# A two-block transformer kernel: raw rows for three units behind each norm of the second block, bias products, another order of PSUM banks

## The chip, the cores and the metric

One Trainium2 chip, one of its cores. The metric is the device time of one launch in microseconds (us), lower is better. All arithmetic is float32; large matrix products are made of float32r products.

## The reference, cut to what matters

A first block (sparse attention, convolution branch, feed-forward network) is followed by a second block of two layers, over 512 tokens of width 1024. The change concerns the norm at the head of each layer of the second block:

```python
for layer in range(2):
    mod = silu(c) @ ada_w[layer] + ada_b[layer]
    shift, scale, gate = split(mod, 3)
    h = rms_norm_2(x, norm_w[layer]) * (1 + scale) + shift
    proj = h @ w_in          # even layer: q, k, v, gates, latents; odd layer: q, k, v, gates
    y = mixer(proj)          # even: two attentions; odd: windowed attention with sinks
    x = x + gate * y
```

For layer 0, `x` is itself the final rms_norm of the first block. Since the inverse root is one number per token, `h @ W` is also `r * ((x * g) @ W) + shift @ W`, with `g` the product of norm weight and `1 + scale` and `r` the inverse root of the token.

## The kernel before, in words

Activations lie transposed: 128 channels on the partitions, 512 tokens along the free axis, eight chunks for the width of 1024 (`xT`). A weight matrix is cut into units of 128 output columns. The list `UNITS` (171 of them) is the order in which SyncE loads them (512 KB each) into five slots of `raw`; the load of a unit waits until the unit five places ahead is done. GpSimd splits each one into `whi` (rounded to float32r) and `wlo` (the rest). TensorE works out a unit in `unit` (L427): for each of eight chunks k a piece of three products of 128x128 by 128x512 (whi by hi, whi by lo, wlo by hi), all into one PSUM bank, 24 products a unit. So the moving side has to be there as a pair hi, lo as well: for the norms `hhi` and `hlo`.

A norm runs over four engines. ScalarE squares each chunk (`square`, L1015, two buffers), VectorE adds the squares up (`add_square`, L1467), TensorE sums them over partitions with `ones` (`sums_of`, L475, one-column products), VectorE and ScalarE make the inverse root (`inverse_root`, L1446; `root`, L1034), TensorE spreads it over the partitions (`spread`, L492), and then VectorE and ScalarE make the rows: `h_split` (L1477) multiplies chunk and gain by the spread root into a PSUM bank (L1485), ScalarE adds the shift and rounds it to `hhi` (`h_high`, L1040), VectorE writes the remainder to `hlo` (L1496). The first unit behind the norm asks for row k before piece k.

Norm "e" of layer 0 stands behind the last "down" products (L687) of the feed-forward network: `double_sums` (L704) sums two vectors, "f" and "e", because the final norm of the first block and the norm of layer 0 are worked out together (VectorE L1915 to L1918 joins them). Four units with their norms on latents follow: ("ecq", 0), ("ecq", 1), ("eckv", 0), ("ekr", 0); then ("eq", 0..3), ("ek", 0), ("ev", 0), ("ega", 0..2), and a loop of 32 attention steps with units as filling (the first is ("ega", 3)). The loop's scores are L773. Tables for the rotary embedding and the latents' matrices (L1265, L1266) are loaded by ScalarE's queue when the last "down" unit is done, and the first rope waits for all of them.

Norm "o" of layer 1 stands behind the eight units "eout". VectorE adds each of them to `xT` (`residual`, L2055) and the squares are added up at once. Then come ("oq", 0..7), ("ok", 0..1), ("ov", 0..1), ("og", 0), and a loop of windowed attention (scores L889) with ("og", 1..7) as filling.

A PSUM bank is taken on TensorE by `Banks.take`: each pool (a tuple of banks) has its own counter, and the next taking of a pool gets the next bank of the tuple; it waits until the last user of that bank, of whatever pool, has freed it. Units use the pool `WIDE` = (0, 1, 2, 3) where nothing else is said: 34 of them before norm "e", 13 between it and the attention loop, then ("eout", 3..7), the "o" units and ("og", 0). ("eout", 0..2) use the pool (0, 1, 2); the scores of both loops (1, 2); the filling units (0,) in the first loop and (0, 3) in the second; sums and spreads `TR` = (4, 5); the rows of h 6 and 7.

The core lines of such a piece, with their order:

```python
for part, (w, x) in enumerate(((whi, hi), (whi, lo), (wlo, hi))):
    m = mm(b[:, :], w[:, s, k * P:(k + 1) * P], x, start=..., stop=...)
```

Of the kernel before, what the change touches and what calls it, by code (L numbers as in the profile page):

```python
# [21 lines left out]
P = 128  # L22
# [89 lines left out]

ROOTS = ("n1", "fe", "o", "z")
# [67 lines left out]
def program(nc, d, out, known):  # L181
    found = {}
    ctx = ExitStack()
    with ctx:  # L184
# [44 lines left out]
        sb("arena_rest", [AB - NR])  # L229
# [82 lines left out]
        sinT = area(T)  # L312
        esg = chunks(area(8 * T), 8)
# [16 lines left out]
        sgr, ropet = hs[:, 0, :], hs[:, 1, :]  # L330

# [86 lines left out]
        def _(pe):  # L418
# [8 lines left out]
            def unit(name, i, src=h_parts, first=None, inline=True, pool=WIDE):  # L427
# [5 lines left out]
                def piece(k):  # L433
# [15 lines left out]
                return piece  # L449

# [24 lines left out]
            def sums_of(name, b, at=0):  # L475

                last = sqt[:, known.get(("sqslot", (name, DC - 1)), 0), :]
                pe.wait_ge(*dve_did.at((name, "acc", DC - 2)))
                for src in (sq_sum[name], last):
                    if src is last:  # L480
                        pe.wait_ge(*sq_ready.at((name, DC - 1)))
                    for tt in range(TT):
                        m = mm(b[:, at + tt:at + tt + 1], src[:, tt * P:(tt + 1) * P], ones[:, 0:1],  # L483
                               start=(src is not last and at + tt == 0), stop=(src is last), skip_group_check=True)
                return m

            def sums_once(name, pool=TR):

                b = bank.take(pe, pool, (name, "sum"))
                sums_of(name, b).then_inc(*pe_did.up((name, "sum")))  # L490
# [213 lines left out]
            def double_sums():  # L704

                b = bank.take(pe, (0,), ("fe", "sum"))
                for half, name in enumerate(("f", "e")):
                    m = sums_of(name, b, half * TT)
                m.then_inc(*pe_did.up(("fe", "sum")))
# [8 lines left out]
            double_sums()  # L718


            spread("e", 0, at=TT)
            spread("f", 0)
# [1566 lines left out]
```

## Time and profile before

| | us |
|---|---|
| median of 3 runs (lowest, highest) | 1392.66 (1387.76, 1399.45) |
| the profiled execution | 1388.33 |
| its span, first to last instruction | 1386.5 |
| mean granted clock of TensorE | 0.98 of 2.4 GHz |

PE is TensorE's products, PEld its weight loads, DVE VectorE, ACT ScalarE, POOL GpSimd, SP SyncE. A row of a timeline gives start, duration, engine, line, operation, output and inputs, shapes and count; in brackets stands the idle time of the engine before it and what ended that. A matmul's duration contains its latency; products follow each other more closely than their durations say. A one-pass product has one record; a float32 product by `ones` or `ident` has two.

### The profile page before, as it was taken

To read this page: it belongs to the slowest core of one execution; us is meant where nothing else is said; L and a number is where in the kernel's file an instruction comes from. 1 tells how busy PE (TensorE), PEld (TensorE's weight loads), DVE (VectorE), ACT (ScalarE), POOL (GpSimd) and SP (SyncE) were. 2 spreads that over 40 slices of the span, in tenths; PEclk is the share of its full clock that TensorE was granted. 3 is DMA by queue.
4 is the path that set the end of the run, shared out by engine and by line. 5 is a ranking of instruction groups with operands and counts; after the bars stand their busy time and mean duration, and the time that the engine had idled before them with its cause. 6 is when DMAs were issued, how large, how long until landed. Compare 5 with 4: busy or idle time off the path is not lost. (4 is left out here: it accounts for less than half of the span.)

```text
span 1386.5 us, 19493 instructions
## 1 busy us (share of the span) xinstructions
PE 1327.6 (96%) x7206; PEld 1040.8 (75%) x7206; DVE 792.5 (57%) x1534; ACT 415.6 (30%) x907; POOL 640.0 (46%) x523
## 2 busy tenths in 40 slices
PE   7999999999999999999999989999999979999996
PEld 6888776688888888888788768776556858766675
DVE  3996778924554777777562354536654251155643
ACT  3011355523121211221110231246665121244521
POOL 5774422236675666666576355632000446622230
PEclk9999999999999999999999989999999989999998
DMA  6431111122353455555543142210000212211111
GB/s 232 149 95 49 59 31 32 31 62 84 99 167 122 159 205 183 198 197 184 180 152 102 46 148 92 76 47 31 1 1 1 82 60 92 91 31 47 32 46 61
DMA packets 37377, 130.23 MB, mean 94 GB/s; under 512 B 4400, under 2 KB 4656, under 8 KB 37040
## 3 DMA queue, kind: packets, MB, share of 16 engines
q1 hardware_dynamic: 27072, 94.16, 21.6%
q10 hardware_dynamic: 10224, 34.94, 6.8%
q8 instruction: 58, 0.95, 0.3%
q14 instruction: 23, 0.19, 0.1%
HBM read 126.98 MB, written 2.10 MB: 93 GB/s over the span
## 5 line engine op out<-in xcount | busy, mean ns | idle before, releaser
L974 POOL TENSOR_TENSOR wlo<-raw,whi 128x1024 fp32r<-128x1024 f32 x171 | 417.6, 2442 | 14.3
L970 POOL TENSOR_TENSOR whi<-raw,ones 128x2 fp32r<-128x2 f32 x171 | 43.1, 252 | 696.1 <-DMA raw<-in_w 696.0
L442 PE MATMUL bank<-hhi,whi 128*128 128x512 f32 x648 | 267.4, 413 | 11.1 <-DVE hlo L1496 4.8
L442 PE MATMUL bank<-ysplit,whi 128*128 128x512 f32 x896 | 277.4, 391 | 0.0
L442 PE MATMUL bank<-hhi,wlo 128*128 128x512 f32 x648 | 255.7, 395 | 0.0
L442 PE MATMUL bank<-hlo,whi 128*128 128x512 f32 x648 | 255.5, 394 | 0.0
L442 PEld LDWEIGHTS bank<-ysplit,whi 128*128 128x128 f32 x896 | 168.2, 188 | 35.8 <-issue 0.8
L971 POOL TENSOR_SCALAR whi<-raw 128x1022 fp32r<-128x1022 f32 x171 | 185.2, 1083 | 0.0
L442 PE MATMUL bank<-ysplit,wlo 128*128 128x512 f32 x448 | 174.7, 390 | 0.0
L442 PEld LDWEIGHTS bank<-hhi,whi 128*128 128x128 f32 x648 | 123.3, 190 | 49.7 <-issue 13.6
L442 PEld LDWEIGHTS bank<-hhi,wlo 128*128 128x128 f32 x648 | 123.5, 191 | 27.2
L442 PEld LDWEIGHTS bank<-hlo,whi 128*128 128x128 f32 x648 | 124.1, 192 | 21.7
L1529 DVE SCALAR_TENSOR_TENSOR arena<-first,arena 128x512 f32<-128x512 f32 x120 | 119.3, 1032 | 0.9
L442 PEld LDWEIGHTS bank<-ysplit,wlo 128*128 128x128 f32 x448 | 84.2, 188 | 17.6
L1220 ACT ACTIVATE arena<-bank,cols 128x512 f32<-128x512 f32 x44 | 34.3, 779 | 177.7 <-DVE bank L1834 177.7
L687 PE MATMUL bank<-hhi,whi 128*128 128x512 f32 x176 | 69.9, 397 | 5.5 <-DVE modp L1818 3.3
L1992 DVE CUSTOM_DVE_ANT_0 arena<-bank,arena 128x512 f32<-128x512 f32 x64 | 44.2, 690 | 48.4 <-PE bank L778 28.9
L1030 ACT ACTIVATE sqt<-xbuf 128x512 f32<-128x512 f32 x40 | 25.3, 632 | 152.0 <-DVE xbuf L2058 72.5
L1329 ACT ACTIVATE arena<-arena,nmax,stat 128x512 f32<-128x512 f32 x64 | 51.6, 807 | 61.2 <-DVE nmax L1999 31.3
L687 PE MATMUL bank<-hlo,whi 128*128 128x512 f32 x176 | 69.7, 396 | 0.0
L687 PE MATMUL bank<-hhi,wlo 128*128 128x512 f32 x176 | 69.7, 396 | 0.0
L1834 DVE TENSOR_TENSOR bank<-bank,arena 128x512 f32<-128x512 f32 x44 | 30.7, 698 | 50.4 <-PE bank L442 50.4
(282 smaller groups left out, 1933.7 us busy)
## 6 DMA issues: line engine op xcount, KB each, us to landing
raw<-in_w SPq DMA_DIRECT2D x171, 512.0 KB, 3.5
arena<-in_ada ACTq DMA_DIRECT2D x48, 512.0 KB, 4.3
xbuf<-in_xT SPq DMA_DIRECT2D x8, 256.0 KB, 4.6
first<-in_w ACTq DMA_DIRECT2D x1, 2048.0 KB, 8.3
xbuf<-in_w ACTq DMA_DIRECT2D x1, 2048.0 KB, 9.2
xbuf<-in_xT ACTq DMA_DIRECT2D x8, 256.0 KB, 4.6
out_t<-xbuf SPq DMA_DIRECT2D x8, 256.0 KB, 2.2
first<-in_uq ACTq DMA_DIRECT2D x1, 768.0 KB, 8.2
```

What stands on the lines that cost most here:

```text
L442: m = mm(b[:, :], w[:, s, k * P:(k + 1) * P], x, start=(k == 0 and part == 0), stop=(k == DC - 1 and part == 2))
L687: m = mm(b[:, :], w[:, u % WS, n * P:(n + 1) * P], x, start=(i == 0 and part == 0), stop=(i == FC - 1 and part == 2))
L970: g.tensor_tensor(whi[:, s, 0:2], raw[:, s, 0:2], ones[:, :], ALU.mult)
L971: g.tensor_scalar(whi[:, s, 2:D], raw[:, s, 2:D], 1.0, 1.0, ALU.mult, ALU.mult)\
L974: g.tensor_tensor(wlo[:, s, :], raw[:, s, :], whi[:, s, :].bitcast(F32), ALU.subtract)\
L1030: A(sqt[:, s, :], src, ACT.Square, scale=scale).then_inc(*sq_ready.up((name, c)))
L1220: A(ua[:, i % 4, :], bank.of(("up", i))[:, :], ACT.Identity, scale=col("ffw", order_up(i) * 3 + 2), bias=col("ffb", order_up(i)))\
L1329: A(abp[:, s % 3, half, :], abp[:, s % 3, half, :], ACT.Exp, bias=nmax[:, x:x + 1], scale=ab_scale(p, half, qt), accum_out=rsum[:, x:x + 1 ...
L1529: V.scalar_tensor_tensor(cacc[:, c, :], z[:, c, k:k + T], w, cacc[:, c, :], ALU.mult, ALU.add)\
L1834: V.tensor_tensor(b[:, :], b[:, :], spread2, ALU.mult).then_inc(*dve_did.up(("un", i)))
L1992: link(V.tensor_tensor_reduce(abp[:, s % 3, half, :], bank.of(("S", "AB", s, half))[:, :], zero, 1.0, -3.0e38, ALU.add, ALU.max, nmax[:, x ...
```

## The change

Each of the two norms gets three units that don't wait for it: the first three behind it read unnormalized rows `x * g` (their pair hi, lo is made on ScalarE and VectorE as soon as a chunk of x is there, in buffers that are free at that time), and the norm's sums and spread are issued by TensorE inside the first and the second of them. Behind each piece, TensorE multiplies the shift (two columns, high and low part) by the same weights, whi and wlo, into bank 3. VectorE then adds the two columns, multiplies the unit's bank by the spread root (a copy of it in SBUF), and ScalarE adds the sum as a bias; what follows is as before. Between these, VectorE and ScalarE make the normalized rows for the remaining units: three, then five. The fourth unit reads them. Table loads on ScalarE's queue move behind the third unit. The double sums use the pool TR. The units of layer 0 use `E_BANKS`, those of layer 1 `O_BANKS`; since pools count by themselves, ("eout", 3..7) and ("og", 0) get other banks of WIDE too.

```diff
+RAW_BANKS, BIAS_BANK = (0, 1, 2), (3,)
+E_BANKS = (3, 0, 1, 2)
+O_BANKS = (3, 0, 1, 2, 3, 0, 1, 2)
+RAW_E, RAW_O = (("ecq", 0), ("ecq", 1), ("eckv", 0)), (("oq", 0), ("oq", 1), ("oq", 2))
...
@@ in unit, behind the three products of piece k
+                    if extra:
+                        m = extra(k, s)
...
+            def bias(tag, layer, j, k, s):
+                if k == 0:
+                    bank.take(pe, BIAS_BANK, (tag, "bias", j))
+                b = bank.tiles[BIAS_BANK[0]]
+                for w in (whi, wlo):
+                    m = mm(b[:, 0:2], w[:, s, k * P:(k + 1) * P], shr[:, layer, k, :],
+                           start=(k == 0 and w is whi), stop=(k == DC - 1 and w is wlo), skip_group_check=True)
+                return m
+
+            def raw_units(tag, layer, units, src, sums_, spread_):
+                def first_extra(k, s):
+                    if k == 4:
+                        sums_(0)
+                    if k == 6:
+                        sums_(1)
+                    return bias(tag, layer, 0, k, s)
+                def second_extra(k, s):
+                    if k == 2:
+                        spread_()
+                    return bias(tag, layer, 1, k, s)
+                unit(*units[0], src=src, first=lambda k: dve_did.at((tag, "rlo", k)), pool=RAW_BANKS, extra=first_extra)
+                unit(*units[1], src=src, pool=RAW_BANKS, extra=second_extra)
+                unit(*units[2], src=src, pool=RAW_BANKS, extra=lambda k, s: bias(tag, layer, 2, k, s))
...
@@ TensorE, norm "e"
-            double_sums()
-            spread("e", 0, at=TT)
-            spread("f", 0)
-            unit("ecq", 0, first=lambda k: dve_did.at(("e", "h", k)))
-            unit("ecq", 1)
+            raw_units("e", 0, RAW_E, raw_e, double_sums, lambda: spread("e", 0, at=TT))
+            unit("ekr", 0, first=lambda k: dve_did.at(("e", "h", k)), pool=TR)
+            spread("f", 0)
             sums("cq", 0, 2)
-            unit("eckv", 0)
             sums("cq", 1, 2)
-            unit("ekr", 0)
-            sums("ckv", 0, 1)
             for c in range(5):
-                unit(*(("eq", c) if c < 4 else ("ek", 0)))
+                unit(*(("eq", c) if c < 4 else ("ek", 0)), pool=E_BANKS)
+                if c == 0:
+                    sums("ckv", 0, 1)
...
@@ TensorE, norm "o"
-            sums_once("o")
-            spread("o", 0)
-            for i in range(DC):
-                unit("oq", i, first=(lambda k: dve_did.at(("o", "h", k))) if i == 0 else None)
+            raw_units("o", 1, RAW_O, raw_o, lambda part: sums_once("o", part), lambda: spread("o", 0))
+            for i in range(len(RAW_O), DC):
+                unit("oq", i, first=(lambda k: dve_did.at(("o", "h", k))) if i == len(RAW_O) else None,
+                     pool=TR if i == len(RAW_O) else O_BANKS)
...
@@ ScalarE
+            def raw_high(tag, c, src, gain, ready):
+                act.wait_ge(*ready)
+                A(src(c)[0], xT[:, c, :], ACT.Copy, scale=gain).then_inc(*act_did.up((tag, "rhi", c)))
+            def rms_copy(tag):
+                act.wait_ge(*pe_did.at((tag, "spread")))
+                A(rsb, bank.of((tag, "spread"))[:, :], ACT.Copy).then_inc(*act_did.up((tag, "rsb")))
+            def raw_add(unit_, x):
+                act.wait_ge(*dve_did.at((*unit_, "scaled")))
+                b = bank.of(unit_)[:, :]
+                A(b, b, ACT.Identity, bias=rawb[:, x:x + 1]).then_inc(*act_did.up((*unit_, "added")))
+                act.wait_ge(*act_did.at((*unit_, "added")))
...
             for i in range(DC):
-                square("f", i, xT[:, i, :], dve_did.at(("x2", i)))
+                raw_high("e", i, raw_e, fgn[:, i:i + 1], dve_did.at(("x2", i)))
+                square("f", i, xT[:, i, :], None)
                 square("e", i, xT[:, i, :], None, scale=col("fg", i))
...
+            raw_add(RAW_E[0], 0)
+            squared("ecq", 0, "cq", 0, ecq[:, 0, :], col("cqg", 0))
+            h_high("e", 0, 3, e_shift)
+            raw_add(RAW_E[1], 1)
+            squared("ecq", 1, "cq", 1, ecq[:, 1, :], col("cqg", 1))
+            h_high("e", 3, DC, e_shift)
             evac("ekr", 0, ekr[:, :])
+            raw_add(RAW_E[2], 2)
+            for dst, name in ((cosA, "cosA"), (sinA, "sinA"), (cosT, "cosT"), (sinT, "sinT"), (uk, "uk"), (uv, "uv")):
+                act.dma_start(dst, d[name]).then_inc(*tabload.up(name, 16))
+            act.dma_start(late[:, 2 * T:2 * T + 1536], d["uq"]).then_inc(*tabload.up("all", 16))
+            squared("eckv", 0, "ckv", 0, eckv[:, :], col("ckvg"))
...
@@ VectorE
+            def raw_low(tag, c, src, gain):
+                hi, lo = src(c)
+                dve.wait_ge(*act_did.at((tag, "rhi", c)))
+                V.scalar_tensor_tensor(lo, xT[:, c, :], gain, hi.bitcast(F32), ALU.mult, ALU.subtract)\
+                    .then_inc(*dve_did.up((tag, "rlo", c)))
+            def raw_scale(tag, unit_, j, x):
+                dve.wait_ge(*unit_done.at(UNIT[unit_]))
+                link(V.tensor_reduce(rawb[:, x:x + 1], bank.of((tag, "bias", j))[:, 0:2], AX_X, ALU.add))
+                bank.freed((tag, "bias", j), dve_did, ("link", dve_did.n - 1))
+                dve.wait_ge(*act_did.at((tag, "rsb")))
+                b = bank.of(unit_)[:, :]
+                V.tensor_tensor(b, b, rsb, ALU.mult).then_inc(*dve_did.up((*unit_, "scaled")))
+            def raw_split(tag, units, x, gain, shift):
+                src = lambda c: xT[:, c, :]
+                raw_scale(tag, units[0], 0, x)
+                h_split(tag, src, gain, shift, 0, 3)
+                raw_scale(tag, units[1], 1, x + 1)
+                h_split(tag, src, gain, shift, 3)
+                raw_scale(tag, units[2], 2, x + 2)
...
             for i in range(DC):
                 residual("eout", i, 0, "x3")
                 if i:
+                    raw_low("o", i - 1, raw_o, gn[:, 1, i - 1:i])
                     add_square("o", i - 1)
-            norm("o", ...)
+            raw_low("o", DC - 1, raw_o, gn[:, 1, DC - 1:DC])
+            dve.wait_ge(*pe_did.at(("o", "sum")))
+            rstd("o", 0, 1.0 / D)
+            raw_split("o", RAW_O, 3, ...)
```

In the down loop, VectorE gets the same `raw_low("e", i - 1, ...)` ahead of its two `add_square`; ScalarE has `raw_high("o", i, ...)` ahead of `square("o", i, ...)`, `rms_copy` behind each `root`, and in the "oq" loop `raw_add`, the copy out, and then rows of h. The shift is split once into `shr` (two small VectorE operations in `modulation`).

## Rows read from the trace of the kernel before

**Rows 1.** The page: TensorE and the others, busy us and share of span
```profile
PE 1327.6 (96%) x7206; PEld 1040.8 (75%) x7206; DVE 792.5 (57%) x1534; ACT 415.6 (30%) x907; POOL 640.0 (46%) x523
```
**Rows 2.** Waits of TensorE by releaser: us in total, times, longest
```profile
PE bank L497 <- DVE stat L1444: 6.2, 4, 1.9
...
PE bank L442 <- DVE arena L1968: 2.1, 1, 2.1
...
PE bank L773 <- DVE arena L1968: 1.5, 1, 1.5
```
**Rows 3.** Table by stretches: us, busy PE, PEld, DVE, ACT, POOL, granted clock, DMA
```profile
796.50:819.60 23.10, 17.75 (x74) 13.53 (x74) 15.56 (x29) 8.36 (x13) 14.20 (x12) 0.70 0.51 188
...
428.00:430.00 2.00, 2.00 (x19) 1.93 (x17) 0.65 (x1) 0.82 (x1) 0.41 (x2) 1.00 0.36 147
...
1210.00:1212.00 2.00, 1.64 (x4) 1.38 (x5) 1.02 (x5) 1.10 (x4) 1.72 (x3) 0.55 0.00 0
```
**Rows 4.** Timeline of TensorE, last down products, and sums behind ("ekr", 0)
```profile
793.53 0.39 PE L687 MATMUL bank<-hhi,wlo 128*128 128x512 f32 x1
...
796.25 0.39 PE L687 MATMUL bank<-hhi,wlo 128*128 128x512 f32 x1
...
837.67 0.95 PE L467 MATMUL bank<-ones,sqt 128*128 128x1 f32 x8
```
**Rows 5.** Timeline of TensorE, last product of eout, first of ("oq", 1)
```profile
1117.64 0.40 PE L442 MATMUL bank<-split_r,wlo 128*128 128x512 f32 x1
...
1140.49 0.40 PE L442 MATMUL bank<-hhi,whi 128*128 128x512 f32 x1
```
**Rows 6.** Timeline of TensorE, small products in a row
```profile
152.74 1.53 PE L561 MATMUL bank<-split_r 128*128 128x64 f32 x12
154.10 0.47 PE L442 MATMUL bank<-hhi,whi 128*128 128x512 f32 x1
...
800.94 1.84 PE L483 MATMUL bank<-ones,sqt 128*128 128x1 f32 x8
```
**Rows 7.** Timeline of VectorE in the down loop and behind the last residual
```profile
793.96 0.69 DVE L1891 TENSOR_TENSOR xbuf<-xbuf,bank 128x512 f32<-128x512 f32 x1 [0.83 <-PE bank L687]
...
1118.74 2.24 DVE L1473 TENSOR_TENSOR arena<-arena,sqt 128x512 f32<-128x512 f32 x1
```
**Rows 8.** Groups by line, 806 to 838: busy us, mean ns | idle before
```profile
L1485 DVE SCALAR_TENSOR_TENSOR bank<-xbuf,fgn,bank 128x512 f32<-128x512 f32 x8 | 5.9, 755 | 2.5 <-PE bank L497 2.3
...
L1046 ACT ACTIVATE hhi<-bank,modc 128x512 fp32r<-128x512 f32 x8 | 5.5, 687 | 8.4 <-DVE bank L1485 8.4
```
**Rows 9.** The largest table load on the page and at its issue; first rope
```profile
first<-in_uq ACTq DMA_DIRECT2D x1, 768.0 KB, 8.2
...
801.75 0.63 ACTq L1266 DMA_DIRECT2D first<-in_uq  x1
...
845.53 0.01 DVE L1932 LOAD_MASK_SELECT arena<-arena  x1 [4.42 <-ACT arena L1272]
```
**Rows 10.** Timeline: first product of ("eout", 3), residual of ("eout", 2)
```profile
1090.20 0.63 PE L442 MATMUL bank<-ysplit,whi 128*128 128x512 f32 x2
...
1090.88 0.75 DVE L2058 SCALAR_TENSOR_TENSOR xbuf<-bank,modc,xbuf 128x512 f32<-128x512 f32 x1
```
**Rows 11.** Timeline: start of the windowed loop, ("og", 1), second scores, a maximum
```profile
1210.36 0.76 PE L442 MATMUL bank<-hhi,whi 128*128 128x512 f32 x1 [2.15 <-DVE arena L1968]
...
1210.53 0.48 DVE L2090 CUSTOM_DVE_ANT_0 arena<-bank,arena 128x256 f32<-128x256 f32 x1
...
1214.11 0.79 PE L889 MATMUL bank<-split_r,ysplit 64*128 64x384 f32 x6
```
**Rows 12.** Timeline: start of the first attention loop, scores 0 and 1, a maximum
```profile
896.26 0.96 PE L773 MATMUL bank<-split_r 64*128 64x512 f32 x6 [1.50 <-DVE arena L1968]
...
898.35 0.69 DVE L1992 CUSTOM_DVE_ANT_0 arena<-bank,arena 128x512 f32<-128x512 f32 x1
...
900.11 0.97 PE L773 MATMUL bank<-split_r 64*128 64x512 f32 x6
```

More of the change, by code:

```diff
@@ L425, in y_parts, with unit @@
                 return yhi(k), ylo(k)
-            def unit(name, i, src=h_parts, first=None, inline=True, pool=WIDE):
+            def unit(name, i, src=h_parts, first=None, inline=True, pool=WIDE, extra=None):
                 u = UNIT[(name, i)]
@@ L473, in stats, with sums_part, sums_once @@
                     sums(name, c, n, src, ready, pool)
[L475 to L484, printed above, removed]
-                return m
-            def sums_once(name, pool=TR):
-                b = bank.take(pe, pool, (name, "sum"))
-                sums_of(name, b).then_inc(*pe_did.up((name, "sum")))
+            def sums_part(name, b, part, at=0):
+                if part == 0:
+                    pe.wait_ge(*dve_did.at((name, "acc", DC - 2)))
+                    src = sq_sum[name]
+                else:
+                    pe.wait_ge(*sq_ready.at((name, DC - 1)))
+                    src = sqt[:, known.get(("sqslot", (name, DC - 1)), 0), :]
+                for tt in range(TT):
+                    m = mm(b[:, at + tt:at + tt + 1], src[:, tt * P:(tt + 1) * P], ones[:, 0:1],
+                           start=(part == 0 and at + tt == 0), stop=(part == 1), skip_group_check=True)
+                return m
+            def sums_once(name, part=None, pool=TR):
+                for x in (0, 1) if part is None else (part,):
+                    b = bank.take(pe, pool, (name, "sum")) if x == 0 else bank.tiles[found[("bank", (name, "sum"))]]
+                    m = sums_part(name, b, x)
+                if x:
+                    m.then_inc(*pe_did.up((name, "sum")))
             def spread(name, c0, pool=TR, at=0):
@@ L702, in _, with double_sums @@
                     m.then_inc(*unit_done.up(u))
-            def double_sums():
-                b = bank.take(pe, (0,), ("fe", "sum"))
+            def double_sums(part):
+                if part == 0:
+                    bank.take(pe, TR, ("fe", "sum"))
+                b = bank.tiles[found[("bank", ("fe", "sum"))]]
                 for half, name in enumerate(("f", "e")):
-                    m = sums_of(name, b, half * TT)
-                m.then_inc(*pe_did.up(("fe", "sum")))
+                    m = sums_part(name, b, part, half * TT)
+                if part:
+                    m.then_inc(*pe_did.up(("fe", "sum")))
             for n in range(DC):
@@ L759, in _ @@
             turn_unit("ev", 0, evtmp)
-            unit("ega", 1)
-            unit("ega", 2)
+            unit("ega", 1, pool=E_BANKS)
+            unit("ega", 2, pool=E_BANKS)
             def ab_scores(s):
@@ L1038, in root, with h_high @@
                 A(stat[:, 0, 0:n], b[:, 192:192 + n], ACT.Sqrt).then_inc(*act_did.up((name, "root")))
-            def h_high(name, n=DC, shift=None):
-                for c in range(n):
+            def raw_high(tag, c, src, gain, ready):
[9 more added lines that the diff above has]
+                act.wait_ge(*act_did.at((*unit_, "added")))
+            def h_high(name, first=0, n=DC, shift=None):
+                for c in range(first, n):
                     act.wait_ge(*dve_did.at((name, "hs", c)))
@@ L1475, in add_square, with h_split @@
                     V.tensor_copy(sq_sum[name], x).then_inc(*dve_did.up((name, "acc", c)))
-            def h_split(name, src, gain, shift=None):
+            def raw_low(tag, c, src, gain):
[10 more added lines that the diff above has]
+                V.tensor_tensor(b, b, rsb, ALU.mult).then_inc(*dve_did.up((*unit_, "scaled")))
+            def h_split(name, src, gain, shift=None, first=0, n=DC + 1):
                 dve.wait_ge(*pe_did.at((name, "spread")))
                 b = bank.of((name, "spread"))
-                for c in range(DC + 1):
+                for c in range(first, n):
                     if c < DC:
```

46 lines of the change are left out of this document (29 added, 17 removed).

## The prediction

> **What bounds the kernel now.** I read the page first. The row of busy times shows TensorE busy for 96% of the span and nobody else above 57% [rows 1]: the reader is to see that time can only be won where TensorE waits, runs at half clock, or is given fewer or shorter products. The waits of TensorE by releaser come second [rows 2]. Two of their lines matter here: the spread matmuls (L497) wait for the reciprocal root, and the scores of both attention loops or the units beside them wait for L1968, the gate's multiply. The table by stretches is third [rows 3]. From the end of the last "down" product to the middle of unit ("ecq", 0), 23.1 us, the granted clock averages 0.70: part of the stretch runs at 2.4 GHz, part at 1.2. So a norm costs its waits and a slow clock behind them.
>
> The size of each hole comes from the timeline of TensorE. Twelve large products take 796.25 - 793.53 = 2.72 us [rows 4], so a unit of 24 takes 5.44. Norm "e": from the end of the last down product, 796.48, to the sum of squares behind ("ekr", 0), 837.67 [rows 4], are 41.2 us. They hold four units (21.8) and the sums of the two halves of cq (1.8, by the price below); the norm costs the other 17.6. Norm "o": from the end of eout, 1117.87, to the first product of ("oq", 1), 1140.49 [rows 5], are 22.6 us with one unit in them; the norm costs 17.2.
>
> **Part 1: what a small product costs.** Each raw unit gets two products with two moving columns behind each of its 8 pieces, 16 a unit, 96 in all. The trace of before has no two-column product of fp32r behind large ones. The nearest is L561: twelve 64-column products, each with a 128x128 fp32r load, and the next large product follows 1.36 us after the first [rows 6], 0.113 each. They are paced by their loads: a large product hides the load of its successor, a small one hides nothing. Two in a row then add 0.227 to each piece of 0.68. From below, the load could be hidden altogether: nothing. From above, the clock could be at its lower level: eight one-column products at 800.94 took 1.84 us [rows 6], 0.23 each. I take 0.113: 96 x 0.113 = 10.9 us (0 to 22.1).
>
> The Trainium skill, "TensorE: Matmul & The Clock Gate", section "Back-to-back issue gap", says that start to start never falls below about 25 ns however few columns a product has. By that floor alone the 96 would be an estimated 2.4 us and the sum 8.5 us better. The rows above speak against using it where every product brings its own weights.
>
> **Part 2: norm "e" afterwards.** TensorE goes from the last down product straight into ("ecq", 0). Its rows are ready: raw_high and raw_low ride in the down loop. There DVE sits idle 0.83 of each 2.72 us [rows 7] and gets one operation more of 0.75 (L1485 is the nearest [rows 8]); ACT gets 0.69 more [rows 8]. Neither overflows. If GpSimd holds DVE up, the last low row comes late: at 1118.74 an add with two SBUF inputs took 2.24 instead of 0.7 [rows 7]. But piece 7 is only asked for 6 us after the down products end, so this is hidden.
> - ecq 0: 5.44 + 16 x 0.113 (1.8) + sums of squares, 32 records x 0.113 (3.6) = 10.9: until 807.4. The sums end about 1.1 before that; the chain of roots takes 1.8 and ends at 808.1.
> - ecq 1: its first bias product needs bank 3 back, which DVE's reduce frees only behind that chain: a wait of 0.5. Then 7.3 plus the spread, 8 x 0.113 = 0.9: until 816.0.
> - DVE and ACT behind the spread (811.2): copy 0.6, scale 0.7, add 0.7, square 0.6, copy out 0.6, first high row 0.69, three rows of h; only then does DVE reduce the second bias, at 817.7. Unit eckv wants the bank at 816.7: a wait of 1.1 to 1.3. It ends at 824.5.
> - ekr reads normalized rows. They come one per 1.44 us (0.75 + 0.75 less an overlap [rows 8]) behind a second interruption of DVE and ACT: row 3 at 822, row 7 at 827.5. ekr wants row 7 at 829.3. No wait. It ends at 829.9.
> - spread "f" and both cq sums: 24 x 0.113 = 2.7: until 832.6, where before it was 837.67.
> So the norm costs 3.6 + 1.8 + 5.4 + 1.8 = 12.6 instead of 17.6: **5.0 us gained**. Its bias products alone take 5.4. The clock stays up in this sum.
>
> The seven table loads move behind the third raw_add on ACT, from about 800 to about 831. The largest was issued in 0.63 and lands 8.2 after issue [rows 9], so I put the last landing near 843. Before, the first rope began at 845.53 after 4.42 us of idleness [rows 9]; the four ropes have 5.44 us or more between arrivals and take 2.9 each. Cost nothing; that cover is gone if the tables land later than about 858, when the fourth rope would miss the heads' root. SP and GpSimd get nothing new, and weight loads stay five units ahead.
>
> **Part 3: norm "o" afterwards.** The same, with one set of sums (16 x 0.113 = 1.8), one spread (0.9), bias 5.4, and shorter chains: DVE is done with the roots at 1127.1 and reduces the first bias by 1127.4, in time for 1127.6; ACT has no squares, so the second is reduced at 1136.2, a wait of 0.6. The last residual ends at 1118.8; behind it come raw_low 6 (2.3 if held up as at 1118.74), the add and raw_low 7, done by 1123 to 1125.5; the sums want the add at 1122.2, piece 7 its row at 1126. Cost 8.7 instead of 17.2: **8.4 gained**. oq 3 then finds its rows: row 7 about 1145.6, wanted about 1147.6.
>
> **Part 4: banks.** The banks in WIDE are dealt by a counter, and 13 units no longer move it: unit eout 3 gets bank 2 instead of 3 and og 0 bank 3 instead of 0.
> - eout 3 finds eout 2 in its bank. TensorE wants it at 1090.20; DVE starts the residual of eout 2 at 1090.88 [rows 10], and now raw_low 0, which itself waits for ACT, comes before it: free at about 1092.45. A wait of **2.25**. After a wait of 2.15 in the C stage the clock was 0.55 and nine products took 1214.11 - 1210.36 = 3.75 instead of 2.05 [rows 3, 11]; I add **1.6**. From below: nothing, if DVE is early.
> - AB scores: before, they waited 1.50 for the last gate [rows 2, 12]. In E_BANKS order they need ega 0 and ega 1 only. What is late next is DVE: scores 1 needs bank 2, read by the maximum at 898.35 + 0.7 [rows 12]. Scores 1 moves from 900.11 to 899.1: **1.0 gained** (0 to 1.5).
> - C stage: og 1 no longer waits for og 0's gate. Before, wait and slow clock put scores 1 at 1214.11 [rows 11]. Now nine products end at 1210.3 and scores 1 waits for the maximum, 1210.53 + 0.48 [rows 11]: 1211.05. **3.0 gained** (2 to 3.75).
>
> **Sum.** 5.0 + 8.4 - 3.85 + 1.0 + 3.0 = 13.5 us. The profiled execution took 1388.3 (span 1386.5 and 1.8 around it), so its like would take 1374.8. The median of the runs shown is 1392.66, 4.3 above that execution; against it the same gain gives 1379. A measurement of this kernel tells about 1% (13.9 us) from no change, so the forecast lies on that line.
>
> **Rivals.**
> - A, the forecast, 1379: 60%. Its own range, with each part's bounds but the small products within a quarter: 1374 to 1385.
> - B, no wait before eout 3, or one too short for the clock to fall: 13.5 + 3.85 = 17.4, **1375**. For it: a 1.50 wait at 896.26 left the following products at their usual spacing (scores to scores 3.85 [rows 12]). Against it: the order of DVE's operations. 15%.
> - C, small products nearly free: the part of 10.9 shrinks to 2.7 (a quarter), gain 21.7, **1371**. For it: the loads of large products are hidden; against it L561 [rows 6]. 6%.
> - D, each two-column product is split in two by the hardware, as those of f32 are (two records each), without a slower clock: 10.9 more, gain 2.6, **1390**. For it: sixteen L483 products per "fe" sum show as 32 records. Against it: L561, also fp32r, shows 12 records for 12. 13%.
> - E, the other side: the clock halves inside the raw units, because so much of their time goes to small products. A large product then takes 0.43 instead of 0.227 and a small one 0.23: a raw unit costs 24 x 0.2 + 16 x 0.117 = 6.7 more. From two such units on the gain is gone. For the three behind norm "e" it is 20.1, gain -6.6: **1399**. For it: at 800.94 the sums already ran at half clock. Against it: sixteen one-column records between large products at 428 kept 1.00 [rows 3], and the slow stretches behind both norms began behind a wait. 6%.
>
> **From these to the numbers.** Faster by over 1% (under 1378.7): nearly half of A, most of B, all of C: 0.46. Slower by over 1%: E, part of its spread: 0.05. The rest, 0.49, is within 1%. Range 1369 to 1391: it takes in A, B, C's upper part and D, and leaves out E.
>
> **What would show it.** Right: no wait of TensorE for L483 and L497 behind these two norms but that of "z" at the end and one of n1 at the start; clock 1.00 from 796 to 850; a raw unit's pieces 0.91 apart; waits of 0.5 and 1.2 (e) and 0.6 (o) before bias products, released by the reduce; a wait of 2.2 before eout 3, released by L2058, with a slow stretch behind it; first AB scores about 6.5 earlier than before. Wrong: pieces 0.7 or 1.14 apart (C or D), a clock of 0.5 in a raw unit (E), a rope waiting for tables, or h rows late for ekr or oq 3.

## The result and the profile after

The changed kernel takes 1378.4 us (median; 1376.92 to 1379.91) against 1392.66 (1387.76 to 1399.45): ratio 0.9904, 95% interval 0.988 to 0.9928. The forecast was 1379. The profiled execution took 1378.68, 9.65 less than that of before, with a span of 1376.9; the sum had promised 13.5 between executions. The page's row of busy times answers to [rows 1]:

```profile
PE 1331.0 (97%) x7302; PEld 1048.5 (76%) x7302; DVE 817.4 (59%) x1564; ACT 430.6 (31%) x931; POOL 641.3 (47%) x523
```

TensorE has 7302 - 7206 = 96 records more, one for each bias product: none is split in two. It is busy 3.4 us longer in a span that is 9.6 shorter. TensorE's waits by releaser, to be held against [rows 2] (us in total, times, longest; L456 is a unit, L473 a bias product, L544 a spread, L527 a sum of squares, L2159 the residual, L1559 the reduce of a bias bank, L818 and L933 the scores of the two loops):

```profile
PE bank L544 <- DVE stat L1516: 2.7, 2, 1.4
...
PE bank L456 <- DVE xbuf L2159: 2.1, 1, 2.1
...
PE bank L527 <- DVE arena L1545: 1.5, 1, 1.5
```

The spreads' wait is 2.7 in two instead of 6.2 in four: those of the norms "e" and "o" are gone. The longest waits for the gate's multiply are gone. New is the 2.1 before ("eout", 3), and 1.5 for the add of squares is that of the last norm.

I cut both profiled executions at the same events and compare the stretches, so that what happens in one does not hide in another. Each number is the start of the one event less the start of the other:

| stretch (us) | before | after | gained | forecast |
|---|---|---|---|---|
| start to last "down" product | 796.25 | 799.85 | -3.60 | 0 |
| to the heads' first sum (norm "e" in it) | 53.21 | 50.75 | 2.46 | 5.0 |
| to scores 1 of the attention loop | 50.65 | 49.62 | 1.03 | 1.0 |
| to the first residual of eout | 188.92 | 187.40 | 1.52 | 0 |
| to the eighth (eout 3 in it) | 29.05 | 32.97 | -3.92 | -3.85 |
| to scores 1 of the second loop (norm "o") | 96.04 | 84.88 | 11.16 | 8.4 + 3.0 |
| to the residual of layer 1 | 119.01 | 118.05 | 0.96 | 0 |
| to the end | 53.39 | 53.34 | 0.05 | 0 |

All terms but one are right to a quarter of a microsecond (those of norm "o" and the C stage, the start of the second loop, 11.4, taken together). Norm "e" gave half. And three stretches that the change does not touch moved by -3.60, +1.52 and +0.96. The table by stretches shows the first of these: in this execution the clock fell at 300, in code equal to that of before, where the stretch had 1.00 (columns: stretch, its length, busy time of PE, PEld, DVE, ACT, POOL, granted clock, DMA share, GB/s):

```profile
300.00:304.00 4.00, 4.00 (x14) 3.42 (x14) 0.16 (x1) 0.00 (x0) 3.24 (x4) 0.50 0.04 12
304.00:308.00 4.00, 4.00 (x14) 3.18 (x13) 0.00 (x0) 0.00 (x0) 0.45 (x1) 0.70 0.00 0
```

**Norm "e".** The timeline of TensorE from the last "down" product (L734) on, in place of [rows 4]:

```profile
799.85 0.39 PE L734 MATMUL bank<-hhi,wlo 128*128 128x512 f32 x1
800.08 0.62 PE L456 MATMUL bank<-ysplit,whi 128*128 128x512 f32 x2
...
802.73 0.72 PE L456 MATMUL bank<-ysplit,whi 128*128 128x512 f32 x2
803.28 0.39 PE L456 MATMUL bank<-ysplit,wlo 128*128 128x512 f32 x1
803.51 0.17 PE L473 MATMUL bank<-shr,whi 128*128 128x2 f32 x1
803.54 0.25 PE L473 MATMUL bank<-shr,wlo 128*128 128x2 f32 x1
803.65 0.71 PE L456 MATMUL bank<-ysplit,whi 128*128 128x512 f32 x2
804.20 0.39 PE L456 MATMUL bank<-ysplit,wlo 128*128 128x512 f32 x1
804.43 1.84 PE L527 MATMUL bank<-ones,arena 128*128 128x1 f32 x16
```

There is no gap behind the "down" products. A piece takes 803.65 - 802.73 = 0.92; without its two small products it would take 0.68 (2.72 for four pieces, [rows 4]). So the two cost 0.24, 0.12 each. Sixteen records of the sums take 806.13 - 804.43 = 1.70. The unit runs from 800.08 to 810.90, 10.8 us. So far all is as forecast. The next lines show what is not (columns as above):

```profile
808.00:812.00 4.00, 3.96 (x27) 3.18 (x26) 1.55 (x9) 0.18 (x1) 3.92 (x4) 0.95 0.02 4
812.00:816.00 4.00, 3.98 (x12) 3.40 (x13) 0.00 (x0) 0.00 (x0) 3.92 (x4) 0.50 0.44 131
816.00:820.00 4.00, 4.00 (x21) 3.69 (x20) 1.75 (x3) 1.59 (x3) 3.92 (x4) 0.70 0.00 0
```

TensorE is busy throughout, waits for nobody, and yet the clock is at 1.2 GHz from about 812 to 818, inside the second raw unit. Behind the second bias bank the wait is shorter than 1.1 to 1.3, because TensorE came late:

```profile
823.78 0.27 PE L473 MATMUL bank<-shr,whi 128*128 128x2 f32 x1 [0.30 <-DVE stat L1559]
```

**eout 3.** VectorE and TensorE, to be held against [rows 10]:

```profile
1089.16 0.75 DVE L1553 SCALAR_TENSOR_TENSOR arena_rest<-xbuf,gn,ysplit 128x512 fp32r<-128x512 f32 x1
1089.83 0.42 DVE L1547 COPY arena<-sqt 128x512 f32<-128x512 f32 x1
1090.16 0.74 DVE L2159 SCALAR_TENSOR_TENSOR xbuf<-bank,modc,xbuf 128x512 f32<-128x512 f32 x1
...
1091.05 0.84 PE L456 MATMUL bank<-ysplit,whi 128*128 128x512 f32 x2 [2.10 <-DVE xbuf L2159]
```

The low row (L1553) goes before the residual that frees the bank, and TensorE waits 2.10. The stretches behind it:

```profile
1092.00:1094.00 2.00, 2.00 (x6) 1.51 (x6) 0.16 (x1) 0.18 (x1) 1.92 (x2) 0.50 0.65 254
1094.00:1096.00 2.00, 2.00 (x9) 1.59 (x8) 0.00 (x0) 0.00 (x0) 2.00 (x3) 0.78 0.00 0
1120.00:1146.00 26.00, 25.72 (x149) 22.12 (x148) 16.05 (x28) 10.50 (x16) 13.27 (x11) 1.00 0.23 69
```

The last row is the whole of norm "o": same raw units, same bias, and the clock stays at 1.00. Its one delay is before the third bias product. The profile gives 0.28 of idle time there, but the piece takes 1.47 instead of 0.92, so 0.55 are lost: an idle time is counted from the end of a product's duration, which contains its latency.

**The two loops.** Scores 1 of the attention loop (L818) and scores 0 and 1 of the second (L933), in place of [rows 12] and [rows 11]:

```profile
900.22 0.98 PE L818 MATMUL bank<-split_r 64*128 64x512 f32 x6 [0.49 <-DVE nmax L2093]
...
1201.88 0.62 PE L933 MATMUL bank<-split_r,ysplit 64*128 64x256 f32 x6 [0.73 <-issue]
...
1205.47 0.80 PE L933 MATMUL bank<-split_r,ysplit 64*128 64x384 f32 x6 [0.70 <-DVE nmax L2195]
```

No gate holds them any longer; the maximum does, for 0.49 and 0.70. Nine products between the scores of the second loop now end before they are wanted.

### The profile page after: what moved, and what is told of

Read it like the earlier page. It is cut to its first block and busy times, and to the rows that moved or that the text cites. A ratio compares the mean times of both kernels' runs of the same rounds, so it can differ in the third digit from the quotient of the medians.

```text
span 1376.9 us, 19734 instructions
## 1 busy us (share of the span) xinstructions
PE 1331.0 (97%) x7302; PEld 1048.5 (76%) x7302; DVE 817.4 (59%) x1564; ACT 430.6 (31%) x931; POOL 641.3 (47%) x523
## 5 line engine op out<-in xcount | busy, mean ns | idle before, releaser
L1018 POOL TENSOR_TENSOR wlo<-raw,whi 128x1024 fp32r<-128x1024 f32 x171 | 418.3, 2446 | 14.3
L456 PE MATMUL bank<-ysplit,whi 128*128 128x512 f32 x968 | 307.6, 397 | 2.1 <-DVE xbuf L2159 2.1
L456 PE MATMUL bank<-hhi,whi 128*128 128x512 f32 x600 | 245.3, 409 | 3.4 <-DVE hlo L1581 3.0
L456 PE MATMUL bank<-hhi,wlo 128*128 128x512 f32 x600 | 236.2, 394 | 0.0
L456 PE MATMUL bank<-hlo,whi 128*128 128x512 f32 x600 | 235.8, 393 | 0.0
L456 PEld LDWEIGHTS bank<-ysplit,whi 128*128 128x128 f32 x968 | 181.1, 190 | 38.3 <-issue 3.2
L456 PE MATMUL bank<-ysplit,wlo 128*128 128x512 f32 x496 | 194.6, 392 | 0.0
L456 PEld LDWEIGHTS bank<-hhi,whi 128*128 128x128 f32 x600 | 113.9, 190 | 34.2 <-issue 9.4
L456 PEld LDWEIGHTS bank<-hhi,wlo 128*128 128x128 f32 x600 | 113.8, 190 | 24.9
L456 PEld LDWEIGHTS bank<-hlo,whi 128*128 128x128 f32 x600 | 114.2, 190 | 20.5
L456 PEld LDWEIGHTS bank<-ysplit,wlo 128*128 128x128 f32 x496 | 93.8, 189 | 20.0
L734 PE MATMUL bank<-hhi,whi 128*128 128x512 f32 x176 | 70.1, 398 | 5.7 <-DVE modp L1915 3.3
L734 PE MATMUL bank<-hhi,wlo 128*128 128x512 f32 x176 | 69.7, 396 | 0.0
L734 PE MATMUL bank<-hlo,whi 128*128 128x512 f32 x176 | 69.7, 396 | 0.0
L1921 DVE SCALAR_TENSOR_TENSOR hlo<-arena,hhi 128x512 fp32r<-128x512 f32 x22 | 35.0, 1591 | 34.8 <-ACT hhi L1294 34.7
```

What stands on the lines that cost most here:

```text
L456: m = mm(b[:, :], w[:, s, k * P:(k + 1) * P], x, start=(k == 0 and part == 0), stop=(k == DC - 1 and part == 2))
L734: m = mm(b[:, :], w[:, u % WS, n * P:(n + 1) * P], x, start=(i == 0 and part == 0), stop=(i == FC - 1 and part == 2))
L1018: g.tensor_tensor(wlo[:, s, :], raw[:, s, :], whi[:, s, :].bitcast(F32), ALU.subtract)\
L1921: V.scalar_tensor_tensor(hlo[:, i % DC, :], fa[:, i, :], 0.5, hhi[:, i % DC, :].bitcast(F32), ALU.mult, ALU.subtract).then_inc(*dve_did.up ...
```

## The experiments

The questions: is the loss at eout 3 the bank alone; do the banks carry what I gave them in the C stage; does a small product cost 0.113; and why did the clock fall in norm "e" and not in norm "o"? For the last there are two theories: the 32 sums records that lie close together behind two pieces ("dense sums"), or chance of phase against something earlier ("phase"). The expectations call the first also S or D, the second R. All stretches below are those of the table.

**The changed kernel once more.**

> The changed kernel once more, as the reference for the others. In its first trace the raw unit (ecq, 1) ran at half clock from 812 to 818, 11.6 us long instead of 8.4. Theory S: it falls because 32 one-column records stand within 6 us in unit (ecq, 0); then this trace shows the same again, clock 0.5 for 5 to 7 us in (ecq, 1). Rival R: the fall came by chance, as one in the first block of that execution (clock 0.68 from 300 to 310); then it is gone here or lies elsewhere. The time: 0.990 of the kernel before, 1377 to 1381 us.

1379.66 us (1378.0 to 1385.76), ratio 0.9926 (0.9898 to 0.9955). Stretches: norm "e" 52.57, eout 32.91, norm "o" with the C stage 84.85. The last two repeat to 0.06; norm "e" took 1.8 more than in the first profile. Its slow stretch is longer and begins earlier, at about 808, still in ("ecq", 0) and ahead of the second lot of sixteen sums records:

```profile
804.00:808.00 4.00, 4.00 (x30) 3.64 (x29) 0.00 (x0) 0.76 (x1) 3.83 (x5) 0.99 0.35 139
808.00:812.00 4.00, 4.00 (x20) 4.00 (x19) 0.52 (x4) 0.00 (x0) 3.92 (x4) 0.50 0.00 0
812.00:816.00 4.00, 4.00 (x12) 3.27 (x12) 1.03 (x6) 0.18 (x1) 3.92 (x4) 0.50 0.32 105
816.00:820.00 4.00, 4.00 (x22) 3.46 (x20) 0.05 (x1) 0.60 (x1) 3.92 (x4) 0.73 0.06 26
```

**Banks of eout and og 0 as they were before.**

```diff
+EOUT_LATE = (3, 0, 1, 3, 2)
-                unit("eout", i, src=e_parts)
+                unit("eout", i, src=e_parts, pool=EOUT_LATE)
-            unit("og", 0)
+            unit("og", 0, pool=(3,))
```

> Units (eout, 3..7) take banks 3, 0, 1, 3, 2, so (eout, 3) no longer waits for bank 2. Theory: the wait of 2.1 us before (eout, 3) is gone and with it the slow stretch behind it (1.7 us): 3.8 us less than the changed kernel, ratio 0.987. Rival: the wait moves to the next unit or to the bias products, or the clock falls all the same: 0 to 2 us less.

1376.93 us (1374.45 to 1383.55), ratio 0.9899 (0.9871 to 0.9927), against 0.987 expected. The eout stretch is 29.04 instead of 32.97: the 3.9 come with the bank and go with it. The wait for L2159 is gone from the list. The profile gave something I had not looked for: norm "e" took 48.25, and the clock stayed up (same stretches of the unit; its "down" products ended 8.7 later):

```profile
812.00:816.00 4.00, 4.00 (x31) 3.69 (x29) 1.00 (x1) 1.59 (x2) 3.92 (x4) 1.00 0.63 230
816.00:820.00 4.00, 4.00 (x31) 3.69 (x30) 0.97 (x6) 0.18 (x1) 3.91 (x4) 1.00 0.02 4
820.00:824.00 4.00, 3.82 (x24) 3.11 (x23) 0.58 (x4) 0.24 (x1) 3.84 (x4) 1.00 0.45 131
```

53.21 - 48.25 = 4.96: this is the term of 5.0 as it was worked out. Up to the first eout the code is that of the changed kernel, so the same instructions take 48.25 in one execution and 52.57 in another.

**The kernel before with the new order of banks alone** (pools of the E and O units, eout and og 0 as in the last run).

```diff
-                unit(*(("eq", c) if c < 4 else ("ek", 0)))
+                unit(*(("eq", c) if c < 4 else ("ek", 0)), pool=E_BANKS)
...
-                unit("ok", i)
+                unit("ok", i, pool=O_BANKS)
```

> The kernel before with nothing but the other order of banks (the units of layer 0 and 1 behind the norms, (eout, 3..7) in 3, 0, 1, 3, 2 and (og, 0) in bank 3). Theory: the second scores of the first loop start 1.0 earlier against the unit before them, those of the second loop 2.9 earlier; 3.9 us less than the kernel before, ratio 0.9972. Rival: the waits come back later in the loops, no gain.

1386.6 us (1383.05 to 1390.1), ratio 0.9968 (0.9951 to 0.9986). Attention loop 49.66 (0.99 gained), norm "o" with the C stage 93.30 instead of 96.04: the banks carry 2.74 there. Scores 1 of the second loop waits as in the changed kernel:

```profile
1213.39 0.79 PE L892 MATMUL bank<-split_r,ysplit 64*128 64x384 f32 x6 [0.69 <-DVE nmax L2093]
```

What is left for norm "o" itself: 93.30 - 84.88 = 8.4.

**Half of the sums.** The sums of squares of "e" are left out, and VectorE reads the sum of "f" in their place, so the output changes. That leaves 16 records instead of 32, eight behind each of the two pieces.

```diff
-                for half, name in enumerate(("f", "e")):
+                for half, name in enumerate(("f",)):
...
-            link(V.tensor_tensor(w, b[:, TT:2 * TT], w, ALU.add))
+            link(V.tensor_tensor(w, b[:, 0:TT], w, ALU.add))
```

> The changed kernel with half of the sums in norm e: only the squares of f are summed (16 records in place of 32), and the sum of e takes their place; this leaves out the sum of the squares of e. Theory S: 1.8 us of products go, and the clock stays at 1.00 through (ecq, 1), 3.2 us more: 5.0 us less than the changed kernel. Rival R (the fall is chance): 1.8 us less in that stretch, and a slow stretch as likely here as there.

1375.69 us (1373.84 to 1379.13), ratio 0.9892 (0.9866 to 0.9918). Norm "e" 46.47, clock 1.00 throughout: 1.78 under 48.25, which is 16 records at 0.111. With half the records there was no fall; one profile can't say more.

This profile also takes the 3.9 of eout 3 apart. The bank is that of the changed kernel, and so is the wait, but here no fall followed: the clock is 1.00 from 1092 to 1100, and the stretch took 31.35.

```profile
1092.06 0.70 PE L456 MATMUL bank<-ysplit,whi 128*128 128x512 f32 x2 [2.10 <-DVE xbuf L2159]
```

So the wait costs 31.35 - 29.04 = 2.3, and the slow clock behind it 1.6 more. The clock fell behind this wait in five of the six profiles that have it.

**The sums dealt out**, eight records behind each of the pieces 4 to 7, instead of sixteen behind 4 and 6.

```diff
-                    if k == 4:
-                        sums_(0)
-                    if k == 6:
-                        sums_(1)
+                    if tag == "e" and k >= 4:
+                        sums_(k)
+                    if tag == "o" and k in (4, 6):
+                        sums_(k // 2 - 2)
...
```

> The changed kernel with the 32 one-column records of norm e dealt over four pieces of (ecq, 0), eight behind each of pieces 4 to 7, in place of sixteen behind pieces 4 and 6. So far the clock fell in (ecq, 1) in two executions of the changed order and stayed up in the one with other banks for eout, whose norm e is the same code. Theory D (dense small products bring it down): spread out, it stays at 1.00; from the last down product to the first head sum 48.5 us (the sums end one piece later). Rival R (the phase of the chip's clock control decides, not the order): 48.5 or 50 to 53, as it happens.

1378.3 us (1377.82 to 1385.29), ratio 0.9927 (0.99 to 0.9955). Norm "e" 49.22 and no slow stretch in it. It is 1 above 48.25; the sums end a piece later, and two bias products wait 1.9 instead of the 1.0 of the run with the eout banks:

```profile
PE bank L473 <- DVE stat L1558: 1.9, 2, 1.1
```

**The sums at once**, all 32 behind piece 6.

```diff
-                    if k == 4:
+                    if k == 4 and tag == "o":
                         sums_(0)
                     if k == 6:
+                        if tag == "e":
+                            sums_(0)
                         sums_(1)
```

> The changed kernel with all 32 one-column records of norm e in one run of 3.6 us behind piece 6 of (ecq, 0). Theory D: the clock falls for certain, from the last down product to the first head sum 51 to 53 us. Rival R: as it happens, 48.3 with the clock up.

1379.93 us (1374.63 to 1380.46), ratio 0.9916 (0.9891 to 0.9941). Norm "e" 49.41, where "dense sums" had said 51 to 53: the clock fell here too, but only for some 3.5 us.

**Each bias product twice** (so the output has the shift doubled).

```diff
-                for w in (whi, wlo):
+                for w, again in ((whi, 0), (whi, 1), (wlo, 0), (wlo, 1)):
...
```

> The changed kernel with every bias product issued twice (the shift of the six raw units counts double, so the output changes), 96 products more. By my price of 0.113 each: a raw piece is 1.13 us long in place of 0.91, and the kernel takes 10.9 us more than the changed kernel, ratio about 0.999. If a load can be hidden once products stand in a row: 0 to 3 us more. If the small products bring the clock down: over 20 us more.

1398.74 us (1394.2 to 1403.16), ratio 1.004 (1.0018 to 1.0063). Pieces in norm "o":

```profile
1141.18 0.47 PE L456 MATMUL bank<-ysplit,whi 128*128 128x512 f32 x1
...
1142.32 0.48 PE L456 MATMUL bank<-ysplit,whi 128*128 128x512 f32 x1
...
1143.45 0.48 PE L456 MATMUL bank<-ysplit,whi 128*128 128x512 f32 x1
```

1.135 apart instead of 0.915: again 0.11 for each small product. Over 48 of them that is 5.3, less what they cover (no wait for the reduce is left there, and the run below puts that at up to 0.6); the stretch with norm "o" grew by 4.70, at clock 1.00 from 1139 to 1165. Norm "e" took 58.58, 10.3 more than the 48.25 at full clock, because there the clock was low for 14 us:

```profile
816.00:820.00 4.00, 4.00 (x20) 3.62 (x18) 0.00 (x0) 0.00 (x0) 3.92 (x4) 0.60 0.00 0
820.00:824.00 4.00, 4.00 (x18) 3.71 (x17) 1.39 (x8) 0.18 (x1) 3.92 (x4) 0.50 0.00 0
824.00:828.00 4.00, 4.00 (x15) 3.42 (x14) 0.16 (x1) 0.00 (x0) 1.40 (x1) 0.50 0.40 131
828.00:832.00 4.00, 4.00 (x22) 3.65 (x21) 0.00 (x0) 0.60 (x1) 3.57 (x3) 0.70 0.00 0
```

So bias products alone, even twice as many, don't bring the clock down in norm "o", which has 16 sums records; beside 32 the fall was longer than in any other profile. The median is 19 to 20 us above the two of the changed kernel, not 10.9; the 96 products more account for some 10 of it at 0.11 each, and in the profile the rest is clock, much of it in code that this edit leaves alone (the part ahead of norm "e" is 8.1 longer than in the first profile of the changed kernel).

**Banks of eout, and a second bank for the third bias.** With the eout banks of above:

```diff
-                    bank.take(pe, BIAS_BANK, (tag, "bias", j))
-                b = bank.tiles[BIAS_BANK[0]]
+                    bank.take(pe, TR if j == 2 else BIAS_BANK, (tag, "bias", j))
+                b = bank.tiles[found[("bank", (tag, "bias", j))]]
...
-            unit("ekr", 0, first=lambda k: dve_did.at(("e", "h", k)), pool=TR)
+            unit("ekr", 0, first=lambda k: dve_did.at(("e", "h", k)), pool=BIAS_BANK)
```

> The kernel with other banks for (eout, 3..7), and the third bias of each norm in a bank of TR in place of bank 3 (the fourth unit behind the norm takes bank 3, the O units 0, 1, 2, 3, 0, 1, 3, 2). Theory: the waits of 0.77 (norm e) and 0.3 to 0.8 (norm o) before the third bias go: 1.1 to 1.5 us less than with other eout banks alone, 5 less than the changed kernel, ratio 0.987. Rival: what waited for the bias bank then waits for the rows of h or for a bank later: no gain.

1374.19 us (1371.14 to 1380.0), ratio 0.9864 (0.9841 to 0.9888). Norm "o" with the C stage 84.29 instead of 84.88: the bias wait there is gone, and with it 0.6, as much as its piece was too long. Norm "e" 51.41, with the clock low.

**Three more, beside each other on one chip:** this version with the sums dealt out, with the sums at once, and as it is.

> The version with the three edits of banks (e6) and the sums of squares dealt out: eight records behind each of pieces 4 to 7 of (ecq, 0) instead of sixteen behind pieces 4 and 6. Theory 'dense sums': the clock falls in the second raw unit because the sums lie in two lumps; dealt out it does not fall: granted clock 1.00 from the last down product to the first head sum, and that interval is 48.3 us; the median is 1 to 2 us under that of the run with the same banks and the old order. Theory 'phase': the same program has the fall in one execution and not in another, whatever the order of the sums; the interval is 48.3 or 51 to 53 with no relation to the edit, and the medians are within 1 us.

1377.46 us (1372.62 to 1383.55), ratio 0.9908 (0.9879 to 0.9937). Norm "e" 47.99, clock 1.00, as "dense sums" had said:

```profile
804.00:808.00 4.00, 4.00 (x30) 3.71 (x29) 0.71 (x1) 1.29 (x2) 3.92 (x4) 1.00 0.52 209
808.00:812.00 4.00, 4.00 (x29) 3.55 (x27) 0.62 (x4) 0.00 (x0) 3.83 (x5) 1.00 0.02 4
```

> The version with the three edits of banks (e6) and all 32 records of the sums of squares behind piece 6 of (ecq, 0). Theory 'dense sums': one lump of 3.6 us is denser than two of 1.8, so the clock falls here for certain and for longer than 4 us: interval from the last down product to the first head sum 51 to 54 us, median 2 us or more above the dealt version. Theory 'phase': as likely with the fall as without it, and the median within 1 us of the two others.

1370.77 us (1370.03 to 1375.73), ratio 0.9849 (0.9821 to 0.9877), the lowest of all. Yet in its profile norm "e" took 49.99, with a slow stretch of some 7 us. "Dense sums" had said 51 to 54 and a worse median; both are wrong. "Phase" had said medians within 1 us of each other; with 1377.46 and 1381.1 beside it that is wrong too. The same order of sums without the banks had no such lead (1379.93), so I don't put it down to the order.

> The very kernel of e6, once more. It was 0.9864 of the kernel before; this should come out at 0.985 to 0.988, some 1373 to 1376 us, if the 5 us over the changed kernel are real. In its first profile the clock fell in (ecq, 1) and the interval from the last down product to the first head sum was 51.4 us. Theory 'dense sums': it falls again in the same unit, 51 to 52.5. Theory 'phase': it may be 48.3 this time, with the clock at 1.00.

1381.1 us (1375.7 to 1385.36), ratio 0.9915 (0.9887 to 0.9943). I had expected 1373 to 1376. The same kernel had 0.9864 (0.9841 to 0.9888) on another chip, so the two intervals only just touch. Norm "e" took 51.43, and its slow stretch began at the same place as in the first profile of this kernel, 8 us behind the last "down" product, in ("ecq", 0):

```profile
812.00:816.00 4.00, 4.00 (x22) 3.67 (x21) 0.00 (x0) 0.00 (x0) 3.92 (x4) 0.69 0.04 12
816.00:820.00 4.00, 4.00 (x16) 3.61 (x17) 1.55 (x9) 0.18 (x1) 3.92 (x6) 0.50 0.00 0
820.00:824.00 4.00, 4.00 (x13) 3.34 (x12) 0.00 (x0) 0.00 (x0) 3.92 (x4) 0.53 0.45 131
```

**What the profiles of norm "e" say together:**

| sums records | stretch with norm "e", us | clock fell |
|---|---|---|
| 16 behind pieces 4 and 6 | 50.75, 52.57, 51.41, 51.43, 48.25 | in 4 of 5, for 7 to 10 us |
| the same, each bias product twice | 58.58 | yes, for 14 us |
| 32 behind piece 6 | 49.41, 49.99 | in 2 of 2, for 3.5 and 7 us |
| 8 behind pieces 4 to 7 | 49.22, 47.99 | in 0 of 2 |
| 8 behind pieces 4 and 6 ("f" only) | 46.47 | no |

Neither theory holds alone. "Phase" is needed for the 48.25. But in norm "o", with 16 sums records in two lots of eight and the same bias, the clock fell in none of the 11 profiles of kernels with raw units, so the sums of norm "e" have a part in it. It is not their number: in four profiles (the second of the changed kernel, both of the kernel with a second bias bank, and that with the bias twice) the clock fell before the second lot had begun, with only sixteen records done. Every profile with a fall has a lot of sixteen or more in a row, with bias products around it; where no lot was longer than eight, the clock never fell. Sixteen in a row without bias products, at 428 [rows 3], had the clock at 1.00 in every profile. That dealing the sums out prevents the fall is what 0 of 2 against 4 of 5 suggests; it is not settled, and no run tells why the same kernel falls in one execution and not in another.

**Which version is best.** By stretches each repair is plain and repeats: 3.9 (eout) and 0.6 (third bias in norm "o"), 4.5 together. By medians no single pair of runs shows it, since the same kernel gave 1374.19 and 1381.1. All executions with the eout repair and both norms complete (five runs, 28 executions) have a mean of 1376.65, those without it (four runs, 20 executions) 1379.71: 3.1 apart, with a standard error of about 1 if the executions are taken as independent; both groups mix the orders of the sums and several chips. So the version of the run with two banks for the bias is better than both kernels by its stretches; the order of its sums is open.

## Why the prediction was right, and where it was not

The total was right: 13.5 forecast against the median of before, 14.3 measured (1392.66 - 1378.4). It lies inside the range of A. The second measurement of the changed kernel, on another chip, gave less: 1390.4 - 1379.66 = 10.7. All 45 executions of before and all 11 of the changed kernel have means 11.9 apart, with a standard error of 0.9. What is missing to 13.5 is no more than the clock took in norm "e" in the two profiles (2.5 and 4.3, below). So the 14.3 flatters the forecast. Between the two profiled executions the same stretches give 13.25 from the last "down" product on, but with terms in it that the forecast had not.

- **What bounds the kernel.** Right: TensorE's waits and the clock behind them were the whole of what was gained; nothing else became the bound.
- **Small products.** Forecast 0.113, measured 0.12 in the changed kernel and 0.11 for doubled ones. The product with its own 128x128 load (L561 [rows 6]) was the right neighbour. The Trainium skill's floor of about 25 ns ("TensorE: Matmul & The Clock Gate", section "Back-to-back issue gap") agrees with the starts of the two bias products of a piece, 0.03 apart (803.51 and 803.54). As a price it is too low: the large products behind them come later, and the piece is 0.24 longer. That ends C, and the count of records ends D.
- **Norm "e".** The sum of 5.0 was right for an execution at full clock: 4.96 in the run with the eout banks. The step that failed is "The clock stays up in this sum". It fell in both profiles of the changed kernel, with TensorE busy and no wait ahead, in ("ecq", 1) in the first and already in ("ecq", 0) in the second, and cost 50.75 - 48.25 = 2.5 and 4.3. So this is rival E in part, and one of the forecast's own signs of being wrong, a clock of 0.5 in a raw unit, did appear: E's mechanism was real, at one place of the two. Its price was near too (a piece at the lower clock took 1.71 instead of 0.92 in the second profile, 6.3 for a whole unit, against 6.7), but the fall lasted 7 and 10 us, less than one unit at that clock, and not through three. The argument against E, the stretch at 428 with sixteen one-column records in a row and 1.00 [rows 3], did not carry to raw units, where bias products lie around the sixteen.
- **Bias waits.** Forecast 0.5 and 1.1 to 1.3 in norm "e", 0.6 in norm "o". The profile gives idle times of 0.2 and 0.8 in norm "e" at full clock and 0.28 in norm "o". By the length of the pieces, which is what the sum was made of, they cost 1.37 - 0.92 = 0.45, 1.95 - 0.92 = 1.03 and 0.55. So these terms were right to 0.1 or so.
- **ekr and tables.** Neither h rows nor tables were waited for, as forecast. The first rope began at 847.74 with VectorE never idle before it for a table.
- **Norm "o".** Forecast 8.4, measured 8.4 by way of the run with banks alone. VectorE was held up as feared (a low row of 1.86 instead of 0.75 at 1121.26), and it was hidden as forecast.
- **eout 3.** Forecast 2.25 of wait and 1.6 of slow clock; measured 2.3 and 1.6, with the help of the one profile in which the clock did not fall. B had two halves: its missing wait never happened, but its wait without a fall did, in that profile.
- **Loops.** 1.0 forecast and 1.03 measured; 3.0 forecast and 2.74 measured with the banks alone.
- **What the sum had no term for.** Differences, by slow stretches, in code that the change does not touch: -3.60 ahead of the norm, 1.52 in the attention loop, 0.96 behind. They came out against each other here (-1.1); in other executions of the same kernel they did not. The median, which the forecast was set against, evens them out better than one profile does. That the two medians gave 14.3 for a sum of 13.5, though the clock took 2.5 or more from norm "e", is luck; the second measurement, 10.7, did not have it.

## What to carry to other kernels

Price a small product that brings its own weights by a neighbour that does so too, not by its columns (0.11 to 0.12 here for 64, 2 and 1 columns), and when units leave a bank counter, follow the counter to every later user of it: 3.9 us of some 17 were lost here in a unit whose own line the change leaves alone. Where a change moves many small products together, put a slow clock into the sum as a term with a chance of its own, even without a wait ahead. When effects are a few us and the clock comes and goes, cut the profiles at common events and compare the stretches; where the clock did the same, they repeat to 0.1 us (29.04 in all six profiles with the eout repair), and medians of the same kernel differ by 7. Check such a gain against a second measurement before calling a forecast exact.

## What had not been expected of the hardware

- The clock fell from 2.4 to 1.2 GHz in a stretch in which TensorE was busy for 3.96 and 3.98 us of 4 (27 records from 808 to 812, then 12 in the next 4 us), for some 7 us. The falls that the forecast had priced all stood behind a wait.
- A wait of 2.10 us before ("eout", 3) was followed by a fall in five profiles and by none in the sixth: 3.9 us lost, or 2.3.
- The same instructions had the fall in one execution and not in another: 48.25 and 52.57 us for norm "e". A place 500 us ahead of the change behaved alike, 0.50 at 300 in the changed kernel and 1.00 in another version with the same code there (the run with the sums at once). Of the attention loop the kernel before shows one at 1068, behind a wait that the changed kernel has too, without the fall:

```profile
1068.00:1072.00 4.00, 4.00 (x20) 3.05 (x17) 0.69 (x1) 0.00 (x0) 0.00 (x0) 0.72 0.00 0
```

- One kernel, measured twice, gave ratios of 0.9864 and 0.9915, on two chips. The interval of one run says how well its own executions agree, not how a second run would come out.
